# A two-layer streaming encoder: the opening stage of its first normalisation and latents reordered

## The reference, cut to what matters

```python
def _rmsnorm(x, g, eps=NORM_EPS):
    y = xf * lax.rsqrt(jnp.mean(xf * xf, axis=-1, keepdims=True) + eps)
    return (y * g.astype(jnp.float32)).astype(x.dtype)
...
    q_lat, kv_lat, kpe_raw, dq, dk, dv = jnp.split(h @ w_in, SPLIT_EVEN, axis=-1)
    ckv = _rmsnorm(kv_lat, g_kv_lora)
    kpe = _rope(kpe_raw, pos)
```

## Time and profile before

| | us |
|---|---|
| median of 3 runs | 1787.08 |
| lowest, highest | 1784.96, 1787.49 |
| the profiled execution, its own time | 1780.77 |
| its span | 1778.9 |

### The profile page before, as it was taken

How to read it: one execution, slowest core, us unless ns; L and a number is a source line. 1 busy time by engine, 2 the same in 40 slices (tenths; PEclk the granted TensorE clock), 3 DMA queues, 4 the chain that set the end, 5 groups by cost and what they waited for, 6 DMA issues and landing times.

```text
span 1778.9 us, 31977 instructions
## 1 busy us (share of the span) xinstructions
PE 1700.0 (96%) x12487; PEld 1634.4 (92%) x12487; DVE 1113.3 (63%) x2058; ACT 803.9 (45%) x1513; POOL 590.4 (33%) x437
## 2 busy tenths in 40 slices
PE   7989999999999899999999999799998999999997
PEld 6878989989998799999999999799988999999997
DVE  5645564555555689478477679533346884884775
ACT  4344554455445555235335444443355551452442
POOL 3333344444544312102102346464453120121122
PEclk9989999999999999999999999899998999999998
DMA  7111131423221223323323142332322242333231
GB/s 205 47 56 44 42 84 47 125 62 83 82 72 54 72 61 108 105 72 96 107 61 101 50 113 63 96 93 67 101 66 73 69 119 71 96 98 93 72 95 54
DMA packets 251849, 145.73 MB, mean 82 GB/s; under 512 B 21678, under 2 KB 241644, under 8 KB 251700
## 3 DMA queue, kind: packets, MB, share of 16 engines
q1 hardware_dynamic: 247080, 135.41, 26.9%
q0 software_dynamic: 3776, 8.03, 1.7%
q10 hardware_dynamic: 844, 0.24, 0.1%
HBM read 130.95 MB, written 15.32 MB: 82 GB/s over the span
## 4 chain that ended last, share of the span: by engine, by line
PE 83%; DVE 9%; ACT 3%; issue 2%; POOL 1%; DMA 1%; ACTq 0%; POOLq 0%; DVEq 0%
PE ACC L1151 40%; PE ACC L1514 7%; PE ACC L1515 7%; PE ACC L1516 7%; PE T L1151 3%; PE S L1388 3%; PE ACC L1413 2%; PE S L1151 2%; DVE SCO L2532 1%; DVE TOP L2529 1%; PE S L1516 1%; PE S L1515 1%; PE S L1514 1%; ACT PR L1892 1%; PE S L1357 1%
## 5 line engine op out<-in xcount | busy, mean ns | idle before, releaser
L2918 POOL TENSOR_TENSOR WL<-RAW,WH 128x1024 fp32r<-128x1024 f32 (+3 forms) x84 | 180.0, 2147 | 197.8 <-ACT WH L1772 197.4
L1151 PE MATMUL ACC<-XGh,WH 128*128 128x288 f32 x1024 | 233.9, 310 | 8.7 <-DVE YK L2392 4.2
L1151 PE MATMUL ACC<-XGh,WL 128*128 128x288 f32 x1024 | 221.2, 298 | 0.0
L1151 PE MATMUL ACC<-XGl,WH 128*128 128x288 f32 x1024 | 220.8, 297 | 0.0
L3055 POOL TENSOR_TENSOR HF<-SG,U 128x576 f32<-128x576 f32 x44 | 64.1, 1456 | 436.1 <-ACT SG L2018 411.1
L1772 ACT ACTIVATE WH<-RAW 128x1024 fp32r<-128x1024 f32 (+3 forms) x159 | 153.1, 970 | 80.3 <-PE ACC L1151 43.7
L1514 PE MATMUL ACC<-TB,WH 128*128 128x288 f32 x640 | 188.7, 295 | 0.6
L1516 PE MATMUL ACC<-TB,WL 128*128 128x288 f32 x640 | 188.6, 295 | 0.0
L1515 PE MATMUL ACC<-TB,WH 128*128 128x288 f32 x640 | 188.3, 294 | 0.0
L1151 PE MATMUL ACC<-HH,WH 128*128 128x288 f32 x1056 | 183.0, 295 | 0.0
L1151 PEld LDWEIGHTS ACC<-XGh,WH 128*128 128x128 f32 x1024 | 164.4, 191 | 14.4 <-DVE YK L2392 5.1
(11 more groups left out here) (421 smaller groups left out, 4402.4 us busy)
## 6 DMA issues: line engine op xcount, KB each, us to landing
RAW<-in_w_gate_dram SPq DMA_DIRECT2D x44, 512.0 KB, 3.9
RAW<-in_w_up_dram SPq DMA_DIRECT2D x44, 512.0 KB, 4.7
RAW<-in_w_down_dram SPq DMA_DIRECT2D x32, 512.0 KB, 3.9
RAW<-in_w_in_even_dram SPq DMA_DIRECT2D x29, 512.0 KB, 5.2
RAW<-in_w_in_odd_dram SPq DMA_DIRECT2D x28, 512.0 KB, 4.6
RAW<-in_w_out_even_dram SPq DMA_DIRECT2D x16, 512.0 KB, 3.9
RAW<-in_w_down_dram SPq DMA_DIRECT2D x16, 384.0 KB, 3.4
MH<-bias_tiles POOLq DMA_DIRECT2D x16, 256.0 KB, 2.9
```

The source lines that it names most:

```text
L1151: ins = pe.matmul(out[0:m, 512 * b:512 * b + width], left, right[:, b * width:(b + 1) * width], start=(first and part == 0), stop=(last an ...
L2918: pool.tensor_tensor(WL[slot][:, 0:n], RAW[slot][:, 0:n], WH[slot][:, 0:n].bitcast(F32), ALU.subtract).then_inc(w_lo_pool, 1)
```

## The change

It touches only the stage above. The gains of the first norm have a semaphore and a transpose of their own; the other seven vectors are turned later. The weights of latent 3 come in two transfers of four tiles each, each half split by itself. Latent 4 starts after four tiles of latent 3 and its high part stands behind x tile 2. The bias inputs are the first thing that GpSimd issues, and the wait for the memsets goes to the end of the stage. The pairs are given by hand: gain, vrow, gv and latent 4 have pair 1, latent 3 has pair 0 to itself.

```diff
-    group("gv")
-    group("vrow")
+    group("gain", use=1)
+    group("vrow", use=1)
+    group("gv", use=1)
...
-    for i in KV_LATS:
+    for n, i in enumerate(KV_LATS):
         unit("lat", i, end=("lat", i))
-        group("lat", i)
+        group("lat", i, use=n)
...
+            def load_first_latent():
+                first = ("lat", KV_LATS[0])
+                view, src = raw_view(first, 0, P), tiles(w_even, 0, DT, P * KV_LATS[0], P)
+                sp.dma_start(view[:, 0:DT // 2, :], src[:, 0:DT // 2, :]).then_inc(lat_in, 16)
+                sp.dma_start(view[:, DT // 2:DT, :], src[:, DT // 2:DT, :]).then_inc(raw_in[slot_of[first]], 16)
             load_x(0)
-            load_unit("lat", KV_LATS[0])
+            load_first_latent()
...
             pe.wait_ge(id_in, 16)
+            pe.wait_ge(gain_in, 16)
+            out = open_pair("gain")
+            pe.transpose(out[0:P, 0:DT], GR[0:DT, :], IDN[0:DT, 0:DT]).then_inc(acc_done, 1)
             turn_x(0)
             turn_x(1)
-            pe.wait_ge(c_in, 16 * 8)
-            out = open_pair("gv")
-            pe.transpose(out[0:P, 0:NG], GR[0:NG, :], IDN[0:NG, 0:NG]).then_inc(acc_done, 1)
-            pe.wait_ge(setup_c, 8)
             pe.wait_ge(b_in, 16 * 2)
             out = open_pair("vrow")
...
-            for i in KV_LATS:
-                open_pair("lat", i)
-            for m in range(DT):
+            def latent_tile(i, m):
+                if m == 0:
+                    open_pair("lat", i)
+                pe.wait_ge(xg_lo, m + 1)
+                if i == KV_LATS[0] and m < DT // 2:
+                    pe.wait_ge(lat_lo, 1)
+                    wh, wl = WH[slot_of["lat", i]], WL[slot_of["lat", i]]
+                else:
+                    wh, wl = unit_ready("lat", i)
+                ins = k_tile(...)
+            first, second = KV_LATS
+            latent_tile(first, 0)
+            latent_tile(first, 1)
+            turn_x(2)
+            turn_x(3)
+            pe.wait_ge(c_in, 16 * 7)
+            out = open_pair("gv")
+            pe.transpose(out[0:P, 0:NG], GR[0:NG, :], IDN[0:NG, 0:NG]).then_inc(acc_done, 1)
+            latent_tile(first, 2)
+            latent_tile(first, 3)
+            latent_tile(second, 0)
+            latent_tile(second, 1)
+            turn_x(4)
+            latent_tile(second, 2)
+            turn_x(5)
+            latent_tile(second, 3)
+            for m in range(4, DT):
                 if m + 2 < DT:
                     turn_x(m + 2)
-                pe.wait_ge(xg_lo, m + 1)
                 for i in KV_LATS:
-                    ...
+                    latent_tile(i, m)
+            pe.wait_ge(setup_c, 8)
...
-            unit_hi(("lat", KV_LATS[0]))
-            act.wait_ge(acc_free, acc.made("gv"))
+            act.wait_ge(lat_in, 16)
+            act.activation(WH[first][:, 0:BLOCK], RAW[first][:, 0:BLOCK], ACT.Copy).then_inc(lat_hi, 1)
+            act.wait_ge(acc_free, acc.made("gain"))
             for m in range(DT):
                 x_tile(m, 0, GOFF[0], (x_taken, m + 1))
                 if m == 0:
+                    act.wait_ge(raw_in[first], raw_value["lat", KV_LATS[0]])
+                    act.activation(WH[first][:, BLOCK:UNIT], RAW[first][:, BLOCK:UNIT], ACT.Copy).then_inc(w_hi, 1)
+                if m == 2:
                     unit_hi(("lat", KV_LATS[1]))
...
+            dve.wait_ge(acc_done, acc.made("gain"))
+            dve.tensor_copy(GV[:, 0:DT], pair(acc.at("gain"))[:, 0:DT]).then_inc(acc_free, 1)
             take_x(0)
-            dve.wait_ge(acc_done, acc.made("gv"))
-            dve.tensor_copy(GV[:, :], pair(acc.at("gv"))[:, 0:NG]).then_inc(acc_free, 1)
-            unit_lo(("lat", KV_LATS[0]))
+            first_latent_lo(lat_hi, slice(0, BLOCK)).then_inc(lat_lo, 1)
             take_x(1)
             x_lo(0, 0)
+            x_lo(1, 0)
+            first_latent_lo(w_hi, slice(BLOCK, UNIT)).then_inc(w_lo, 1)
             dve.wait_ge(acc_done, acc.made("vrow"))
             dve.tensor_scalar(VROW[:, :], ...).then_inc(acc_free, 1)
+            take_x(2)
+            take_x(3)
+            x_lo(2, 0)
+            x_lo(3, 0)
             unit_lo(("lat", KV_LATS[1]))
-            for m in range(2, DT):
-                take_x(m)
-                x_lo(m - 1, 0)
+            dve.wait_ge(acc_done, acc.made("gv"))
+            dve.tensor_copy(GV[:, DT:NG], pair(acc.at("gv"))[:, DT:NG]).then_inc(acc_free, 1)
+            take_x(4)
+            for m in range(4, DT):
+                if m + 1 < DT:
+                    take_x(m + 1)
                 if m == 6:
                     begin("lat", KV_LATS[0])
-            x_lo(DT - 1, 0)
+                x_lo(m, 0)
...
+            pool.dma_start(OH[:, :], a["onehot"]).then_inc(b_in, 16)
+            pool.dma_start(TAB[:, :], a["rel_bias_table"]).then_inc(b_in, 16)
             pool.memset(ONES[:, :], 1.0).then_inc(setup_c, 1)
...
-            pool.dma_start(TAB[:, :], a["rel_bias_table"]).then_inc(b_in, 16)
-            pool.dma_start(OH[:, :], a["onehot"]).then_inc(b_in, 16)
```

More of the change, by code:

```diff
@@ L710, in build @@
         x_in = [sem(f"x_in{i}") for i in range(XPARTS)]
+        gain_in, lat_in, lat_hi, lat_lo = sem("gain_in"), sem("lat_in"), sem("lat_hi"), sem("lat_lo")
         id_in, c_in, b_in, lam_in, rope_in, cc_in = (sem(n) for n in ("id_in", "c_in", "b_in", "lam_in", "rope_in", "cc_in"))
@@ L1243, in _ @@
             pe.matmul(out[0:HEADS, SEQ:REL], TAB[:, :], OH[:, SEQ:REL], start=True, stop=True).then_inc(acc_done, 1)
-            for i in KV_LATS:
-                open_pair("lat", i)
-            for m in range(DT):
+            def latent_tile(i, m):
[7 more added lines that the diff above has]
+                    wh, wl = unit_ready("lat", i)
+                ins = k_tile(pair(acc.at("lat", i)), wh, wl, m * P, P, XGh[:, m, :], XGl[:, m, :], m == 0, m == DT - 1)
+                if m == DT - 1:
+                    ins.then_inc(acc_done, 1)
+            first, second = KV_LATS
[15 more added lines that the diff above has]
+            for m in range(4, DT):
                 if m + 2 < DT:
                     turn_x(m + 2)
-                pe.wait_ge(xg_lo, m + 1)
                 for i in KV_LATS:
-                    wh, wl = unit_ready("lat", i)
-                    ins = k_tile(pair(acc.at("lat", i)), wh, wl, m * P, P, XGh[:, m, :], XGl[:, m, :], m == 0, m == DT - 1)
-                    if m == DT - 1:
-                        ins.then_inc(acc_done, 1)
+                    latent_tile(i, m)
+            pe.wait_ge(setup_c, 8)
             pe.wait_ge(x_taken, DT)
@@ L1823, in _ @@
                 n = g.shape[0] // P
-                act.dma_start(GR[at_row:at_row + n, :], g.rearrange("(m p) -> m p", p=P)).then_inc(c_in, 16)
+                act.dma_start(GR[at_row:at_row + n, :], g.rearrange("(m p) -> m p", p=P)).then_inc(c_in if at_row else gain_in, 16)
                 at_row += n
-            unit_hi(("lat", KV_LATS[0]))
-            act.wait_ge(acc_free, acc.made("gv"))
+            first = slot_of["lat", KV_LATS[0]]
+            act.wait_ge(lat_in, 16)
+            act.activation(WH[first][:, 0:BLOCK], RAW[first][:, 0:BLOCK], ACT.Copy).then_inc(lat_hi, 1)
+            act.wait_ge(acc_free, acc.made("gain"))
             for m in range(DT):
@@ L2279, in _, with first_latent_lo @@
             link(dve.tensor_scalar(IDB[:, :], IDN[:, :], BIG, None, ALU.mult))
+            def first_latent_lo(hi, cols):
+                slot = slot_of["lat", KV_LATS[0]]
+                dve.wait_ge(hi, 1)
+                return dve.tensor_tensor(WL[slot][:, cols], RAW[slot][:, cols], WH[slot][:, cols].bitcast(F32), ALU.subtract)
+            dve.wait_ge(acc_done, acc.made("gain"))
+            dve.tensor_copy(GV[:, 0:DT], pair(acc.at("gain"))[:, 0:DT]).then_inc(acc_free, 1)
+            dve.wait_ge(acc_free, acc.made("gain"))
             take_x(0)
-            dve.wait_ge(acc_done, acc.made("gv"))
-            dve.tensor_copy(GV[:, :], pair(acc.at("gv"))[:, 0:NG]).then_inc(acc_free, 1)
-            dve.wait_ge(acc_free, acc.made("gv"))
-            unit_lo(("lat", KV_LATS[0]))
+            first_latent_lo(lat_hi, slice(0, BLOCK)).then_inc(lat_lo, 1)
             take_x(1)
             x_lo(0, 0)
+            x_lo(1, 0)
+            first_latent_lo(w_hi, slice(BLOCK, UNIT)).then_inc(w_lo, 1)
             dve.wait_ge(acc_done, acc.made("vrow"))
             dve.tensor_scalar(VROW[:, :], pair(acc.at("vrow"))[0:HEADS, 0:REL], 1.0 / DIFF_SCALE, None, ALU.mult).then_inc(acc_free, 1)
+            take_x(2)
+            take_x(3)
+            x_lo(2, 0)
+            x_lo(3, 0)
             unit_lo(("lat", KV_LATS[1]))
-            for m in range(2, DT):
-                take_x(m)
-                x_lo(m - 1, 0)
+            dve.wait_ge(acc_done, acc.made("gv"))
[4 more added lines that the diff above has]
+                    take_x(m + 1)
                 if m == 6:
                     begin("lat", KV_LATS[0])
-            x_lo(DT - 1, 0)
```

(2 more changed lines are left out.)

## The result

| | before | after |
|---|---|---|
| median, us (20 runs each) | 1785.22 | 1789.39 |
| lowest, highest | 1780.71, 1787.68 | 1785.34, 1794.88 |
| the profiled execution, its own time | 1780.77 | 1791.08 |
| its span | 1778.9 | 1789.2 |
| the mark (start of the kp product) | 35.02 | 40.21 |

The ratio of the two is 1.003 [1.002, 1.004]: the changed kernel is **slower**, by 4.2 us between the medians and by 5.4 by the ratio. The fastest runs say the same (1785.34 against 1780.71). The forecast was 1787.5, no change in 0.83 of the cases, and it gave "slower" 0.07. That 1789.39 lies inside its range (1783.3 to 1790.4) is in part luck: the range was laid around the median of three runs, 1787.08, and twenty runs of the same kernel have 1785.22.

What follows compares the result with a forecast made beforehand. TensorE, busy for 96% of the span, was taken as the bound, with time won only where it waits or runs at half clock. Stage -0.2 plus clock +0.6 gave +0.4 us on 1787.08: 1787.5, range 1783.3 to 1790.4.

Steps and rivals of the forecast that it cites:

- then the lead goes: Stage from about 14 us: some five microseconds won by then are lost as TensorE waits for low parts.
- the slow spell from about 18: TensorE near 18 us: its clock falls in about half of the cases, costing 1.7 us at most.
- the term for the clock: TensorE in the stage: a possible clock fall near 18, set against an early first rise; mean +0.6 us.
- So the stage ends 0.2 us earlier: End of the stage: kp product at 34.8, before 35.0, with the clock's possible fall left out.
- the replay: The changed stage worked through queue by queue with instruction prices from the earlier trace; it put the mark at 34.8.
- the first rise can come at 11.5 and not 18: TensorE at the stage's start: the clock reaches 2.4 GHz early, a gain already counted in the stage's -0.2 us.
- a fall and no early rise, +2.5: TensorE's clock in the stage: the slow end of the estimate, +2.5 us, where the sum taken was +0.4.
- The landings: Start of the stage: the first gains land at about 5, before x at 5.74, and cost nothing.
- rival D: Head of TensorE's queue: the gains land late; at 8 us the mark comes 2 to 3 us later; chance 0.07.
- The exclusion of VectorE and GpSimd: Low parts of x on VectorE: each is blocked until a running GpSimd addition of 1.42 us is over.
- part 3: Bias inputs first on GpSimd: one-hot lands at 6.9, memsets about 1 us later harm nobody; landing at 9.4 costs one microsecond.

Runs made afterwards that it cites:

- the fillers: The changed kernel with 28 more products that nobody reads, placed where TensorE waited; mark 38.11, ratio to the kernel before 1.0015.

## Why the prediction was right and wrong

**Right: the mechanism.** "By here the kernel is some five microseconds ahead" (4.5), "then the lead goes", the waits for low parts of x at tiles 2 and 3, the one for the second latent's low part, the slow spell from about 18, and that a shift passes from stage to kernel: all are in the traces. Another order of the same work, and nothing else, moves the mark by 7.1 us, and this names the cause: the products stand in front of the turnings that feed the other engines. That the lead goes at the second latent's high part on ScalarE is only a small part of it: moved away, it brought the second latent 0.4 earlier, and the rest of the 2.3 in that mark is the clock.

**Wrong: the sizes, and first of all the term for the clock.** "So the stage ends 0.2 us earlier", plus 0.6 for the clock, gave +0.4; the mark moved by +5.2. Step by step, against the replay's own times:

| | replay | trace | late by | what is added |
|---|---|---|---|---|
| turning 0 | 5.74 | 6.55 | 0.8 | landing of x and gains |
| tiles 0 and 1 done, turning 2 | 12.5 | 14.5 | 2.0 | the two tiles at 1.2 GHz |
| tile 2 | 15.7 | 17.9 | 2.2 | |
| tile 3 | 18.0 | 20.1 | 2.1 | |
| second latent | 19.2 | 22.5 | 3.3 | its low part 2.43, not 1.2 |
| tile 4 | 26.0 | 31.3 | 5.3 | the second latent's tiles 0 to 2 and turning 4 at 1.2 GHz |
| the mark | 34.8 | 40.2 | 5.4 | |

1. **The clock term**, the largest. The replay had the two first latent tiles at full speed ("the first rise can come at 11.5 and not 18"). It came just before 14.8, and in the second profile of this kernel near 27.5. The first latent's two tiles took 3.05 us (11.46 to 14.51), not 1.8: 1.2 us. And the fall was priced over a stretch as long as that of the earlier trace rows, 3.4 us, "1.7 at most", in half of the cases. It lasted 10.2 us with TensorE busy for 9.07; worth 2.1 by the fillers. With both, the term is 3.3 us in place of a mean of +0.6. The 3.4 us were a misreading as well: the rows stop at 90.0, but the spell does not. TensorE before:

```profile
92.45 0.68 PE L1151 MATMUL ACC<-QGh,WL 128*128 128x288 f32 x2
```

At 92.45 a pair still takes 0.68, so that spell was nearly seven microseconds long, twice what was carried over. My own other end, "a fall and no early rise, +2.5", was nearer to what happened than the sum that I took.
2. **The landings**: "then it is before x (5.74) and costs nothing". The gains came at 6.12 and x at 6.55. I asked when the small transfer would land and not what the one-hot and table, asked for first, do to the first quarter of x. 0.7 to 0.8 us at turning 0, of which 0.2 was left at tile 2 when they were asked for late. By my own sign, turning 0 after 5.8 stood for rival D, and it came at 6.55; but D priced gains that land at 6.12 at under one microsecond, and no more was lost by it.
3. **Low parts of weights.** The exclusion of VectorE and GpSimd was applied to the low parts of x, where the trace before showed it, and not to those of the weights. The second half of the first latent took 1.90 beside an addition (12.12 to 13.58) where the first half alone took 0.68, and the second latent's 2.43. The Trainium skill, "SBUF — State Buffer", section "SBUF: two separate sides", has it for any VectorE operation with two SBUF inputs; these rows agree with it, and I had narrowed the rule to one kind. 1.2 us in front of the second latent. No run takes this away by itself: with the high part behind tile 3 it still took 2.31, and with turnings ahead, where it began before the addition, 1.22, and the addition took 1.70 in place of 1.4.

The one-hot was there in time and the memsets' shift cost nothing, as part 3 said, but part 3 had nothing to win: in the kernel with the inputs late, the bias row starts earlier.

**The chances.** "Slower" had 0.07, all of it for rival D, a late landing that decides from 8.5. The landing was late by 0.8 and the loss came by another way: two smaller errors, and a clock that cost more than both (3.3 against 0.8 and 1.2). The replay's error was taken from how well it gave the order before (34.8 for 35.02). But its free choices, the clock's rise above all, had been fitted there, and nothing said that they would hold for an order with gaps in other places.

## What to carry to other kernels

In a queue in which one engine both prepares inputs for the others (turnings) and uses what they give back, put the preparing ahead by as many tiles as the way round takes; useful work in front of it feels like a gain where it starts and is paid for later. Price a gap of TensorE at itself plus a low clock over what follows for as long as the worst spell of the trace, and not the shortest. Where whole runs scatter by as much as the effect, compare a mark at the end of the changed stage. And before a shift of the mark is put down to an edit, look where the clock rose and fell in both profiles: the first rise moved by some 13 us between two profiles of one kernel.

## What the runs showed of the hardware

- **Work without gaps did not bring the fast clock by itself.** With turnings ahead, TensorE worked from 6.5 without a gap worth naming (turnings, bias row, products in between), and pairs took 0.68 until about 17; with the first latent in one load, a turning took 0.99 at 20.54. In the changed kernel the clock came up before 14.8, in its second profile near 27.5. Nine identity products from 3.43 had it up by 7.6 (a turning's four transposes 0.65 and not 1.11). What sets this was not settled.
- **Low spells last differently** after the same kind of gap: about 3.4 us (two turnings moved), 6.8 us (bias inputs late), 10.2 us (changed kernel), none (the kernel before at 262 us after a wait of 3.35, where the changed kernel had 6.8 us). TensorE was busy for most of each.
- **Small transfers asked for first go with a later first large one**: in the three kernels that ask for one-hot and table late, turning 0 starts at 5.66 to 5.84, and in nine that ask for them first (the two with products in front of it aside) at 6.39 to 6.60. The one-hot took 4.8 us to land when asked for first and 6.2 in the kernel before.
- **VectorE's low parts of weights double beside a GpSimd addition**: 128x1024 took 1.23 and 1.22 in the kernel before, 2.43 and 2.31 where an addition had begun just ahead (changed kernel; high part behind tile 3).
